# Experts of a two-layer encoder in plain fp32 on unsplit weights, on four column quarters of the array

## What is computed

```python
N_EXPERTS, TOP_K, EXPERT_DIM = 8, 2, 3584

def swiglu(h, w_gu, w_down):
    gu = h @ w_gu                      # w_gu: 1024 x 7168
    g, u = jnp.split(gu, 2, axis=-1)
    return (jax.nn.silu(g) * u) @ w_down   # w_down: 3584 x 1024

def moe_swiglu(h, w_router, w_gu, w_down):
    ...
    top_val, top_idx = lax.top_k(logits, TOP_K)
    top_w = jax.nn.softmax(top_val, axis=-1)
    ...
    for e in range(N_EXPERTS):
        out = out + gates[:, e:e + 1] * swiglu(ht, w_gu[e], w_down[e])
```

## Time and profile before

| | us |
|---|---|
| median of three runs | 1623.32 (1620.71 to 1627.07) |
| the profiled execution | 1619.01 |
| its span, first to last instruction | 1617.2 |
| TensorE busy (share of the span) | 1564.7 (97%) |
| VectorE busy | 1253.9 (78%) |
| ScalarE busy | 1040.3 (64%) |
| mean transfer rate | 291 GB/s |

### The profile page before, as it was taken

One profiled execution on the slowest core, in us unless ns is written; L12 is line 12 of the kernel. 1 busy time (PEld: TensorE's weight loads), 2 busy tenths in 40 slices (PEclk: granted clock), 3 DMA queues, 4 the chain that ended last, 5 costly groups with the idle time before them and its releaser, 6 DMA issues.

```text
span 1617.2 us, 22085 instructions
## 1 busy us (share of the span) xinstructions
PE 1564.7 (97%) x8329; PEld 1320.6 (82%) x8329; DVE 1253.9 (78%) x1047; ACT 1040.3 (64%) x921; POOL 113.6 (7%) x127
## 2 busy tenths in 40 slices
PE   6999999999999998999999999999999999999997
PEld 5888889999788886887887887887887887888875
DVE  4866775545686586888888888888888888888896
ACT  4455653333545665778778778778778778777774
POOL 5402000100320005000000000000000000001000
PEclk9999999999999999999999999999999999999999
DMA  9645446655554276999999999999999999999980
GB/s 289 204 137 118 162 164 235 239 190 187 166 183 131 87 289 250 399 395 382 384 367 366 382 368 365 382 367 365 383 367 365 382 368 365 383 367 365 395 317 28
DMA packets 226464, 470.37 MB, mean 291 GB/s; under 512 B 9024, under 2 KB 62816, under 8 KB 226400
## 3 DMA queue, kind: packets, MB, share of 16 engines
q1 hardware_dynamic: 222816, 458.29, 78.7%
q0 software_dynamic: 2176, 6.29, 1.6%
q10 hardware_dynamic: 1408, 4.92, 0.8%
HBM read 462.66 MB, written 11.01 MB: 293 GB/s over the span
## 4 chain that ended last, share of the span: by engine, by line
PE 84%; DVE 7%; ACT 4%; issue 2%; DMA 1%; POOL 1%; SPq 0%; ACTq 0%; DVEq 0%; POOLq 0%
PE bank L1400 27%; PE bank L1401 26%; PE bank L1402 26%; DVE w_slot_lo L448 3%; ACT w_hi L441 3%; PE bank L1697 1%; DMA w_slot<-in_w_in 1%; PE bank L1450 1%; PE bank L1464 1%; PE bank L1435 1%; ACT L959 0%; ACT L441 0%; DVE neg_max L1107 0%; PE bank L1658 0%; PE bank L1648 0%
## 5 line engine op out<-in xcount | busy, mean ns | idle before, releaser
L448 DVE TENSOR_TENSOR w_slot_lo<-w_slot,w_hi 128x2048 fp32r<-128x2048 f32 x429 | 979.1, 2293 | 237.2 <-ACT w_hi L441 236.1
L441 ACT CAST w_hi<-w_slot 128x2048 fp32r<-128x2048 f32 x429 | 815.8, 1906 | 305.4 <-PE bank L1402 293.2
L1400 PE MATMUL bank<-w_hi,a_lo 128*128 128x512 f32 x1208 | 481.5, 399 | 16.4 <-DVE w_slot_lo L448 10.0
L1401 PE MATMUL bank<-w_slot_lo,a_lo 128*128 128x512 f32 x1208 | 476.1, 394 | 0.0
L1402 PE MATMUL bank<-w_hi,a_lo 128*128 128x512 f32 x1208 | 474.2, 393 | 0.0
L1400 PEld LDWEIGHTS bank<-w_hi,a_lo 128*128 128x128 f32 x1208 | 228.2, 189 | 74.2 <-DVE w_slot_lo L448 18.5
L1402 PEld LDWEIGHTS bank<-w_hi,a_lo 128*128 128x128 f32 x1208 | 227.6, 188 | 50.9
L1401 PEld LDWEIGHTS bank<-w_slot_lo,a_lo 128*128 128x128 f32 x1208 | 228.0, 189 | 45.7
L1400 PE MATMUL bank<-w_hi,b_lo 128*128 128x512 f32 x448 | 177.0, 395 | 0.4 <-DVE b_lo L1310 0.4
L1401 PE MATMUL bank<-w_slot_lo,b_lo 128*128 128x512 f32 x448 | 175.9, 393 | 0.0
L1402 PE MATMUL bank<-w_hi,b_lo 128*128 128x512 f32 x448 | 175.2, 391 | 0.0
(11 more groups left out here) (167 smaller groups left out, 1209.6 us busy)
## 6 DMA issues: line engine op xcount, KB each, us to landing
w_slot<-in_moe_w_gu SPq DMA_DIRECT2D x224, 1024.0 KB, 5.4
w_slot<-in_moe_w_down SPq DMA_DIRECT2D x112, 1024.0 KB, 5.1
w_slot<-in_w_in SPq DMA_DIRECT2D x44, 1024.0 KB, 5.1
w_slot<-in_ffn_w_gu SPq DMA_DIRECT2D x22, 1024.0 KB, 5.1
w_slot<-in_ffn_w_down SPq DMA_DIRECT2D x11, 1024.0 KB, 4.9
w_slot<-in_w_out SPq DMA_DIRECT2D x8, 1024.0 KB, 5.0
w_slot<-in_w_branch SPq DMA_DIRECT2D x8, 768.0 KB, 4.5
picked_rows<-in_constants ACTq DMA_DIRECT2D x4, 1024.0 KB, 7.4
```

Source lines behind the costliest of these rows:

```text
L441: nc.scalar.copy(hi_slot[n % HI_RING][:, 0:WIDTH[n]], raw[:, 0:WIDTH[n]]).then_inc(hi_ready, 1)
L448: eng.tensor_tensor(lo, raw, hi, ALU.subtract).then_inc(lo_ready, 1)
L1400: nc.tensor.matmul(place, lhs[0], rhs[0], start=first, stop=False)
L1401: nc.tensor.matmul(place, lhs[0], rhs[1], start=False, stop=False)
```

## The change

**Places.** 96 places for each expert instead of 128, in three groups of 32 tokens (`TOKEN_GROUPS`).

**Plain fp32.** The experts' weights are no longer split. TensorE waits for a tile's transfer alone and multiplies the raw fp32 tile with raw fp32 tokens. ScalarE's casts and VectorE's subtractions of expert weights, and the splitting of tokens and activations, are gone.

**Four column quarters.** A matmul has 32 stationary columns (one token group) and writes to 32 PSUM partitions, that is to one column quarter of the array. For each weight chunk and each `b` of three, `units` gives four matmuls on the four quarters: the three token groups, in quarters 0 to 2, all with weight stream `b`, and token group `b` in quarter 3 with weight stream 3. So after three `b`, all three groups have met all four streams. A gate or up tile is one chunk of 128 rows by 1792 columns (0.917 MB, in runs of 7 KB): half of the 3584 hidden columns (`PARTS` = 2), as four streams of 448. Down tiles are two chunks by 1024 columns (1.05 MB), or, for the chunk that lies across the two halves, one chunk of 0.52 MB that comes by two transfers. An expert has 32 gate and up tiles and 16 down tiles. The order is gate, up for the first half, gate, up for the second, then all of down, with four streams of 256 columns into banks 6, 7 and 2.

**Around them.** The ring has 16 slots; two of them take over the buffers of `w_hi`. ScalarE takes three SiLUs per half, VectorE three products, TensorE transposes three blocks for each chunk, and VectorE copies them out. The last expert's table of places is built by plain fp32 matmuls in the middle of its first product, and its result is scattered by 20 matmuls in place of 8; the token's weight is now applied when the rows are added. The second and third rounds are written out and run only if an expert has more than 96 tokens.

```diff
-SLOTS = 128
+SLOTS = 96
...
-MOE_RING = 14
 HI_RING = 3
-SCATTER_BANKS = (2, 3, 6, 7)
+
+
+TOKENS = 32
+TOKEN_GROUPS = SLOTS // TOKENS
+STREAMS = 4
+PARTS = 2
+STREAM = EXPERT_DIM // STREAMS // PARTS
+PART = STREAMS * STREAM
+Y_STREAM = D_MODEL // STREAMS
+CHUNKS = EXPERT_DIM // STREAMS // P
+PART_CHUNKS = (range(0, STREAM // P), range(STREAM // P, CHUNKS))
+SPLIT_CHUNK = STREAM // P
+MOE_RING = 16
+SCATTER_BANKS = (3, 4, 5, 2)
...
+def down_tiles():
+
+    tiles = []
+    for part, js in enumerate(PART_CHUNKS):
+        js = [j for j in js if j != SPLIT_CHUNK]
+        if part:
+            tiles += [((s, SPLIT_CHUNK),) for s in range(STREAMS)]
+        tiles += [((s, js[0]), (s, js[1])) for s in range(STREAMS)]
+        tiles += [((s, js[2]), (s + 1, js[2])) for s in range(0, STREAMS, 2)]
+    return tiles
+
+
+DOWN = down_tiles()
+Y_ORDER = (2, 0, 1)
...
+    for part in range(PARTS):
+        for kind in "gu":
+            tiles += [(kind, part, c) for c in range(DC)]
+    return tiles + [("d", t, 0) for t in range(len(DOWN))]
+
+
+def units(b):
+
+    return [(g, g, b) for g in range(TOKEN_GROUPS)] + [(TOKEN_GROUPS, b, STREAMS - 1)]
...
-        w_hi = sb("w_hi", HI_RING * TILE, F32R)
+        w_hi_raw, w_hi = sb_split("w_hi", HI_RING * TILE)
...
+        raw_slot = [raw[:, :] for raw, _ in slots] + [w_hi_raw[:, s * TILE:(s + 1) * TILE] for s in range(2)]
...
+                if kind != "d":
+                    col = t * PART + (EXPERT_DIM if kind == "u" else 0)
+                    sp.dma_start(raw_slot[slot][:, 0:PART], moe_w_gu[0, e][c * P:(c + 1) * P, col:col + PART])\
+                        .then_inc(slot_landed[slot], 16)
+                    return
+                w = moe_w_down[0, e].rearrange("(g r) n -> r g n", r=STREAM)
+                (s, k), *other = DOWN[t]
+                if not other:
+                    half = STREAM - SPLIT_CHUNK * P
+                    sp.dma_start(raw_slot[slot][0:half, 0:D_MODEL], w[STREAM - half:, s, :]).then_inc(slot_landed[slot], 16)
+                    sp.dma_start(raw_slot[slot][half:P, 0:D_MODEL], w[0:P - half, STREAMS + s, :]).then_inc(slot_landed[slot], 16)
+                    return
+                part, row = divmod(k * P, STREAM)
+                g = part * STREAMS + s
+                if other[0][0] == s:
+                    src = w[row:row + 2 * P, g, :].rearrange("(c p) n -> p c n", p=P)
...
+                    src = w[row:row + P, g:g + 2, :]
+                sp.dma_start(raw_slot[slot].rearrange("p (c n) -> p c n", c=2), src).then_inc(slot_landed[slot], 16)
...
                     sp.wait_ge(w_used, ND - DENSE_RING + dense_order.index(slot) + 1)
                 elif slot < DENSE_RING + attn_slots:
                     sp.wait_ge(oT_ready, DEPTH * NV)
+                elif slot >= MOE_RING - 2:
+                    sp.wait_ge(w_used, ND)
...
-            split.moe(0, 2)
...
+                for part in range(PARTS):
+                    act.wait_ge(w_used, moe_used(item, MOE_PLACE[("g", part, DC - 1)]))
+                    for b in range(TOKEN_GROUPS):
+                        nc.scalar.activation(act_rows[b][:, part * STREAM:(part + 1) * STREAM], bank[b][:, 0:STREAM],
+                                             ACT.Silu).then_inc(silu_done, 1)
...
+                    act.wait_ge(w_used, moe_used(item, MOE_PLACE[("u", PARTS - 1, DC - 1)]))
+                    picked_out(item + 1)
...
+                def act_product(part):
+                    dve.wait_ge(w_used, moe_used(item, MOE_PLACE[("u", part, DC - 1)]))
+                    for b in range(TOKEN_GROUPS):
+                        dve.wait_ge(silu_done, item * (PARTS * TOKEN_GROUPS) + (part * TOKEN_GROUPS + b + 1))
+                        v = act_rows[b][:, part * STREAM:(part + 1) * STREAM]
+                        nc.vector.tensor_tensor(v, v, bank[3 + b][:, 0:STREAM], ALU.mult).then_inc(act_ready, 1)
+
+                def act_out(part):
+
+                    n = len(PART_CHUNKS[part])
+                    for b in range(TOKEN_GROUPS):
+                        dve.wait_ge(actT_done, item * (PARTS * TOKEN_GROUPS) + (part * TOKEN_GROUPS + b + 1))
+                        v = bank[3 + b][:, 0:n * P].rearrange("p (j t) -> p j t", t=P)
+                        nc.vector.tensor_copy(actT[part][:, b, :, :], v[:, :, 0:SLOTS])
+                        nc.vector.tensor_copy(actT[part][:, STREAMS - 1, :, b * TOKENS:(b + 1) * TOKENS], v[:, :, SLOTS:P])\
+                            .then_inc(actT_ready, 1)
...
-            def moe_tile(item, kind, f, half, chunks):
-                j = MOE_PLACE[(kind, f, half)]
-                n = ND + j
-                pe.wait_ge(lo_ready, item * MOE_TILES + (n + 1))
-                return parts(n, moe_slot(j), chunks, TILE)
+            def moe_tile(item, kind, t, c):
+
+                j = MOE_PLACE[(kind, t, c)]
+                pe.wait_ge(slot_landed[moe_slot(j)], landed(item, j))
+                return raw_slot[moe_slot(j)]
...
+                def up(kind, part, after=None):
+
+                    first_bank = 3 * "gu".index(kind)
+                    for c in range(DC):
+                        w = moe_tile(item, kind, part, c)
+                        if kind == "g" and part == 0 and c == 0:
+                            pe.wait_ge(picked_ready, item * 2 + 2)
+                            if not first:
+                                pe.wait_ge(banks_read, (on_chip(item) - 1) * 4)
...
+                        for b in range(TOKEN_GROUPS):
...
+                            for g, i, s in units(b):
+                                last = nc.tensor.matmul(bank[first_bank + b][g * TOKENS:(g + 1) * TOKENS, 0:STREAM],
+                                                        pickedT[:, c, i * TOKENS:(i + 1) * TOKENS],
+                                                        w[:, s * STREAM:(s + 1) * STREAM], start=c == 0, stop=c == DC - 1)
                         last.then_inc(w_used, 1)
...
+                        if after is not None and c == 2:
+                            after()
...
+                def act_transposes(part):
+                    js = PART_CHUNKS[part]
+                    for b in range(TOKEN_GROUPS):
+                        pe.wait_ge(act_ready, item * (PARTS * TOKEN_GROUPS) + (part * TOKEN_GROUPS + b + 1))
+                        for n, j in enumerate(js):
+                            last = nc.tensor.transpose(bank[3 + b][:, n * P:(n + 1) * P], act_rows[b][:, j * P:(j + 1) * P], ident)
+                        last.then_inc(actT_done, 1)
...
+                def down(t):
+                    w = moe_tile(item, "d", t, 0)
+                    if t == 0:
+                        if first:
+                            pe.wait_ge(y_copied, item * 2 + 2)
+                        pe.wait_ge(silu_done, (item + 1) * (PARTS * TOKEN_GROUPS))
+                    part = 0 if DOWN[t][0][1] in PART_CHUNKS[0] else 1
+                    if len(DOWN[t]) == 1 and DOWN[t][0][0] == 0:
+                        pe.wait_ge(actT_ready, (item + 1) * (PARTS * TOKEN_GROUPS))
+                    final = t == len(DOWN) - 1
+                    for b in Y_ORDER:
+                        for n, (k, j) in enumerate(DOWN[t]):
+                            for g, i, s in units(b):
+                                col = n * D_MODEL + s * Y_STREAM
+                                last = nc.tensor.matmul(y_place(b)[g * TOKENS:(g + 1) * TOKENS, :],
+                                                        actT[part][:, k, j - PART_CHUNKS[part][0], i * TOKENS:(i + 1) * TOKENS],
+                                                        w[:, col:col + Y_STREAM], start=t == 0 and n == 0,
+                                                        stop=final and n == len(DOWN[t]) - 1)
...
+                up("g", 0, places if scatters else None)
+                up("u", 0)
+                up("g", 1, lambda: act_transposes(0))
+                up("u", 1)
+                for t in range(len(DOWN)):
+                    down(t)
+                    if t == 1:
+                        act_transposes(1)
+                    if t == 3 and more:
+                        if first:
+                            picked_transposes(item + 1)
+                        else:
+                            gather(item + 1)
```

400 lines of the change are left out of this document (148 added, 252 removed).

## The result

The changed kernel took 1627.9 us (median; 1624.3 to 1634.8), the kernel before 1621.3 us beside it: a ratio of 1.0041, with a 95% interval of 1.0031 to 1.0052. The interval lies above 1, so the kernel is some 0.4% slower; that is within the 0.5% that the prediction counts as no change. The forecast of 1573 us and of a faster kernel was wrong. The rest of this document is about where some 55 us went.

The account below looks back on a forecast made before the run. TensorE bounds it, the transfer close behind. First matmul 635.2, eight experts 909.6, seven jumps 7, table 2.2: last matmul 1554.0; tail 5.2, end 7.5: span 1566.7; plus 1.8 and 4.3: 1573 us, range 1555 to 1592 (0.66).

Parts of the forecast that it names:

- What bounds the kernel before: Expert loop, 121.35 us per expert: the period is TensorE's, with the transfer close behind.
- The four quarters run together: Gate, up and down: four streams at full rate, 0.376 and 0.215 us a step; slower rival 0.05, 0.05 and 0.08.
- 2.38 for three column tiles: Rival in gate, up and down: 79% of full use, steps 1.26 times as long, kernel near 1798 us.
- TensorE's sum: TensorE per expert: gate and up 72.2, down 36.1, transposes 3.2, quarter switches 1.2, gaps 1.0; sum 113.7 us.
- The way back: Jump back in TensorE's expert loop: a fetch costs 0 to some 3 us; 1 us taken for each of seven.
- The transfer: Weight DMA during the experts: 390 GB/s plus the ring's reserve suffices, break-even 378 GB/s; nothing charged.
- the forecast's own rival: Weight DMA becomes the bound under 378 GB/s: at 372, 14 us more, 1587; chance 0.12 for 1580 to 1640.
- the parenthesis at the end of the paragraph on the transfer: Four half-size tiles, two 64-partition DMAs each: at half rate 5 us an expert, 43 in all; could cost 15.
- 358 GB/s per core: Skill's HBM limit on the weight DMA: last weights at 1595 us, kernel ending near 1617; trace said to disagree.
- The edges: Around the experts: first matmul at 635.2 us, last expert's table and switch 2.2, tail 5.2, then 7.5 to the end.
- The other rivals: Clock: quarters at the lower level, about 2440 us, chance 0.02; second round: everything again, about 910 us, no chance.

Follow-up runs that it names:

- straight version: The changed kernel with the first round's loop over seven experts written out on TensorE, ScalarE, VectorE and SyncE, so nothing jumps back: 1604.6 us, ratio 0.988 to the kernel before.
- interleaved straight version: The straight version with each half-size down tile's two 64-row pieces interleaved over 128 partitions, brought by one transfer, same output: 1553.6 us, ratio 0.958 to the kernel before.
- version with other rows: The straight version with each half-size down tile loaded by one transfer of 128 consecutive rows, not the needed ones, so output differs: 1550.8 us, ratio 0.957.

## Why the prediction was wrong, step by step

**What bounds the kernel before** was read rightly, and so was the warning that the transfer is close behind TensorE.

**The four quarters run together: right,** though this was the step with the least support. In the chain 312 records of gate and up, 78 steps, take 29.45 us, and 480 of down, 120 steps, take 26.04: 0.378 and 0.217 us a step, against 0.376 and 0.215 predicted. The Trainium skill, "TensorE: Matmul & The Clock Gate", section "Measured speedup vs the span model", has 2.38 for three column tiles, which the prediction weighed; four of them do better here, they give full use.

**TensorE's sum: right within 1.5 us.** Without pauses an expert takes 112.23 us, against 113.7: gate and up 42.84 + 29.45 = 72.3 (predicted 72.2), down 26.04 + 5.18 + 5.32 = 36.5 (36.1), transposes 1.13 + 1.46 + 0.81 = 3.4 (3.2). Nearly all of the 2.2 us for gaps and for switching into and out of the quarters was not there. Over eight experts that is 12 us less than predicted.

**The way back: the step that failed.** The prediction saw that an expert's body grows from 1,080 records to 2,940 and priced a jump back that has to fetch at "between 0 and some 3 us", with "1 us for each of seven turns" in the sum. There are six, and each costs 12.95 us: 78 us in place of 7. Two errors are in it. The bound came from a row on another engine at the end of the program, where nothing was waited for behind the jump but one DMA; it is no upper end for a pause of TensorE. And the pause was priced without the clock: of the 12.95 us, 8.8 are the two pauses and about 4 are TensorE at its lower level, a cost that the earlier trace rows could have shown, since there too it was granted 0.50 behind the routing's pauses. What makes the pauses as long as they are stays open.

The Trainium skill names this stall. "Runtime: NRT & Kernel Launch", section "Instruction fetch mechanics", gives TensorE's instruction memory as 2,048 instructions and says that a taken branch to a target outside the current window of two pages waits for a fetch. The runs agree with the first figure as far as they go: 1,080 records are held, 2,160 are not. With a window of two pages they do not agree: by the section's 256 instructions a page that would be an estimated 512, and 1,080 are held.

**The transfer: charged nothing, and right for the change as it stands,** where TensorE never waits for a tile. But this only holds because the pauses give the DMA 78 us. In the straight version the forecast's own rival came true: by it, 367 GB/s make 1587 + 12, some 1600 us; the straight version brought 367 and took 1604.6. So with the ways back at nothing the forecast would have missed too, above its range of 1555 to 1592. The cause stood in the parenthesis at the end of the paragraph on the transfer. There the half-size tiles were put at 5 us of DMA time an expert, with 15 us left to show. Measured they take 10 to 11 us an expert, and 54 us show. Where no way back and no slow tile is left the rest of the sum comes out: 1573 less 7 for the ways back and 12 for the experts is 1554, and the interleaved straight version took 1553.6.

The Trainium skill bears on this in "SBUF — State Buffer", section "Door 1: The DMA port swizzle": partitions 0 to 63 reach half of the sixteen ports and 64 to 127 the other half. The trace agrees, with 238 to 260 GB/s in the windows shown where 128 partitions bring 389 or 396. The Trainium skill, "DMA: Bandwidth & Descriptors", section "Rules for kernel authors", says that two transfers to disjoint halves serialize even from two queues, and that a first dimension under 16 confines a transfer to at most that many engines. The traces agree with both (259 GB/s; share 0.14). The 358 GB/s per core of the section "Where 436 GB/s comes from" on the same page of the Trainium skill, weighed in the prediction, is not a bound here, where one core ran: the version with other rows brought 385 GB/s over the 900 us from 640 to 1540.

**The edges** were 3 us short in all. The first expert's first matmul starts at 637.12, where 635.2 was predicted. The end of the chain, against the earlier trace rows:

```profile
1594.90 19.47 PE bank L1730 x360
...
1619.31 0.75 DVE x_sb L1328
```

From the last weight matmul's end (1614.37) to that of the last addition (1620.06) are 5.7 us, where 5.2 were predicted, and from there to the end of the span 8.2 in place of 7.5. A sum of the parts as measured closes the account: 1566.7 us of predicted span, less 12 for the experts, plus 71 for the ways back, plus 3 for the edges, is 1629; the span was 1628.3.

**The other rivals** did not occur: in the version with other rows the granted clock is 1.00 over the 900 us from 640 to 1540, so plain fp32 on quarters keeps the upper level when nothing interrupts it.

## What to carry to other kernels

When a change makes a loop's body longer in instructions, look at the instruction queue's bytes and count the ways back: a body that was held and no longer is costs each turn a pause, here about 1 us with large matmuls and 9 us with small ones, plus the low clock behind the long ones. Writing the loop out is the test. Price a pause on TensorE with that clock. When two engines or an engine and the transfer are within a few per cent of each other, a stall on one pays for the other: of the 74 us that both together gave (1553.6), taking away one alone gave 23 (1604.6) or 9 (1618.8). And bring each tile in by a transfer that reaches all 128 partitions and whose first dimension is not small (64 brought 396 GB/s, 2 brought 55), even if rows have to be permuted for it.

## What the runs showed of the hardware beyond that

- A DMA whose first dimension is 2 kept some two of sixteen engines busy (share 0.14): 55 GB/s, and 237 us more for the straight kernel, in which each expert had four of them.
- Half of the partitions from a second queue at the same time brought nothing (259 against 260 GB/s) and cost 11 us.
- The first pause at a way back has the same length for 2,938 and for 5,876 records in the body (4.8 to 5.1 us), and is 0.7 to 1.3 us for 2,160 and 3,240 records of larger matmuls. Only the body of 2,938 has a second one.
- The second pause fell from about 3.9 to 2.5 us when the slow transfers went and the DMA share in it fell from 0.50 to 0.80 to 0.24 to 0.37; the first, at a share of 1.02, did not change.
- A loop whose body is not held moves about as many bytes of instructions as the same loop written out (2.31 and 2.06 MB).
